# Ending and beginning each stage of a diffusion transformer in two token halves

## The chip, the cores and the metric

The kernel runs on one core of one Trainium2 chip. The metric is the device time of one execution in microseconds (us). The core's engines work side by side from queues of their own, each in order: TensorE (PE in the profile, its weight loads PEld), VectorE (DVE), ScalarE (ACT), GpSimd (POOL), and SyncE (SP), which issues the DMAs. They meet at semaphores.

## The reference

Two layers over 512 latent tokens `h` and 256 context tokens `hc`, 1024 features each. Every layer has three residual stages, and each begins with an RMS norm over the features, scaled and shifted by vectors that a product with `w_ada` gives:

```python
h  = h + 0.5 * g1 * swiglu(modulate(rms_norm(h, p['g_ffn1']), s1, sc1), w1_gate, w1_up, w1_down)
qa, ka, va, qb, kb, vb, uf = split_mixer_inputs(modulate(rms_norm(h, p['g_mix']), s2, sc2) @ p['w_in'])
o  = concatenate([window_attention(...), global_attention(...), fourier_mix(uf, w_four)]) @ p['w_out']
h  = h + g2 * o
h  = h + 0.5 * g3 * swiglu(modulate(rms_norm(h, p['g_ffn2']), s3, sc3), w2_gate, w2_up, w2_down)
# the same for hc, except that after the last layer's mixer only h goes on; the result is rms_norm(h, g_final)
```

## The kernel before

Activations lie with features on the partitions and tokens in the columns: `h`, `xh` and `xl` are 128 partitions x 8 feature blocks (KD) x 768 tokens (TOK: 512 latent, SEQ, then 256 context). For accuracy every product is made of three in a rounded format: a value is its rounded part (`xh`, `whi`, `ah`) plus the rest (`xl`, `wlo`, `al`), and hi x hi, lo x hi and hi x lo are added up in PSUM (`product`, L1234). For one feature block and 768 tokens that is six matmuls: 512 and 256 columns, three times. Each has its own weight load.

There are six stages n = 0 to 5: ffn1, mix, ffn2 in each layer. An ffn stage has two groups g. A group makes 11 pairs of gate and up tiles (8 feature blocks each) and then 8 down tiles d (11 blocks each). A mixer makes 12 tiles of `w_in`, the Fourier part and attention, and 8 tiles of `w_out`. The last stage, and `w_out` of the second layer, work on 512 tokens only. PSUM has two accumulators `ring[0]` and `ring[1]` for these tiles in turn, `side` for small things and two banks. `slot_free` makes TensorE wait until the tile two before has been read.

Weights come through two slots. SP loads `raw` (`load_w`, L319), ACT rounds it to `whi` (`split_hi`, L585) once the product that used the slot has ended (`mm_done`), VectorE makes `wlo` (`split_lo`, L886). After each down or `w_out` tile VectorE adds it to `h` (`residual`, L979), ACT squares the new block (`square`, L604) and GpSimd adds squares up in `acc` (`sum_squares`, L447; the last block is left to TensorE).

A stage's norm stands between the last tile and the next stage's first pair: TensorE sums acc and the last square over the partitions with one-column fp32 matmuls (`sum_chunks`, L1253), ACT takes the root, VectorE the inverse and lays it on diagonals (`norm`, L934; ACT's part is L610), TensorE spreads them to all partitions by a product with ones (`spread_rstd`, L1262), and for each of 8 blocks VectorE makes `t1` (L967), ACT adds the shift and rounds to `xh` (L632), VectorE makes `xl` (L975). `product_pair` (L1238) takes the first two tiles together, block by block as `x_ready` allows, and both end with the last block. In an ffn stage the third tile's split waits for that end. In a mixer the small `wf` products (L1129) and head squares (L1062) follow the pair; `wf` is zeroed by GpSimd and loaded by SP once the whole of x is made (L343 to L348), for it lies where `t1` was.

The `ada` work (L592, L892, L1270) makes the modulation vectors of later stages in 84 halves of units. Plan puts them in slots of ffn stages 0, 2 and 3: a slot is one pair or one down tile (L99 to L108). `gates` (L923) turns a part of them into the factors that `residual` uses.

## Time and profile before

| | us |
|---|---|
| median of 3 runs (2939.7 to 2941.72) | 2941.56 |
| the profiled execution | 2938.7 |
| its span, first to last instruction | 2936.9 |
| TensorE busy | 2764.7 (94%) |
| VectorE, ScalarE, GpSimd busy | 1506.7, 1005.9, 669.7 |

The mean granted clock of TensorE is 0.976 of its full rate. A matmul's duration in the trace holds the time to pass through the array, so matmuls overlap, and the distance of two starts is what one costs in a row.

### The profile page before, as it was taken

What the parts mean: (1) busy time and instruction counts of PE and PEld (TensorE: products, weight loads), DVE (VectorE), ACT (ScalarE), POOL (GpSimd) and SP (SyncE); (2) the same over time, 40 slices, a digit from 0 to 9 for tenths busy, and PEclk for the clock granted to TensorE, in tenths of its full rate; (3) what the DMA queues carried; (4) which work ended last, traced back from release to release, by engine and by line L of the source; (5) the groups of instructions that cost most, each with busy time, mean ns of one, the idle gap of its engine ahead of it and who ended that gap; (6) DMA issues with size and microseconds to landing.
All of it is one profiled execution on the core that took longest, in us unless ns stands there. A gap on an engine that the chain in (4) does not pass through costs nothing.

```text
span 2936.9 us, 36842 instructions
## 1 busy us (share of the span) xinstructions
PE 2764.7 (94%) x14988; PEld 2333.2 (79%) x14988; DVE 1506.7 (51%) x2075; ACT 1005.9 (34%) x1569; POOL 669.7 (23%) x563
## 2 busy tenths in 40 slices
PE   6999999999877889999999899999998987899998
PEld 2888888878656778888888788888887766788886
DVE  1556655664387455565557555422224577433333
ACT  2333333333376333332334333111213366322231
POOL 1233323433033212343325132100011223100001
PEclk8999999989999989999999999999998999999999
DMA  5333333414320123333333233212212520233232
GB/s 214 101 107 132 110 111 108 133 50 157 99 48 15 37 69 115 113 127 109 101 122 115 75 104 111 78 51 65 66 64 78 160 51 1 65 100 108 84 104 78
DMA packets 69432, 274.34 MB, mean 93 GB/s; under 512 B 8592, under 2 KB 9872, under 8 KB 68240
## 3 DMA queue, kind: packets, MB, share of 16 engines
q1 hardware_dynamic: 69264, 271.99, 29.2%
q8 instruction: 119, 1.95, 0.3%
q14 instruction: 49, 0.40, 0.0%
HBM read 258.85 MB, written 13.11 MB: 93 GB/s over the span
## 4 chain that ended last, share of the span: by engine, by line
PE 88%; DVE 6%; ACT 3%; issue 2%; DMA 1%; SPq 0%; POOL 0%; DVEq 0%; ACTq 0%; POOLq 0%
PE ring L1234 74%; PE ring L1248 3%; PE bank L1196 2%; PE side L1177 2%; PE side L1109 1%; PE bank L1301 1%; ACT pth L672 1%; PE bank L1192 1%; PE bank L1280 1%; DVE rstd L882 1%; DVE rstd L880 1%; DVE wlo L889 1%; PE ring L1158 1%; DVE ptl L869 1%; PE ring L1163 1%
## 5 line engine op out<-in xcount | busy, mean ns | idle before, releaser
L1234 PE MATMUL ring<-xh,whi 128*128 128x512 f32 x2808 | 788.4, 349 | 19.5 <-DVE wlo L889 15.9
L1234 PE MATMUL ring<-xh,wlo 128*128 128x512 f32 x2808 | 785.1, 348 | 0.0
L1234 PE MATMUL ring<-xl,whi 128*128 128x512 f32 x2808 | 783.0, 347 | 0.0
L889 DVE TENSOR_TENSOR wlo<-raw,whi 128x1024 fp32r<-128x1024 f32 (+1 forms) x280 | 390.7, 1395 | 551.7 <-ACT whi L590 551.6
L1234 PEld LDWEIGHTS ring<-xh,whi 128*128 128x128 f32 x2808 | 447.0, 189 | 92.9 <-issue 19.1
L1234 PEld LDWEIGHTS ring<-xl,whi 128*128 128x128 f32 x2808 | 446.1, 189 | 70.6
L1234 PEld LDWEIGHTS ring<-xh,wlo 128*128 128x128 f32 x2808 | 446.1, 189 | 70.2
L445 POOL TENSOR_TENSOR ada_acc<-ada_acc,ada_tmp 128x384 f32<-128x384 f32 x252 | 336.1, 1334 | 529.2 <-ACT ada_tmp L602 508.7
L590 ACT ACTIVATE whi<-raw 128x1024 fp32r<-128x1024 f32 (+1 forms) x280 | 314.4, 1123 | 208.1 <-PE ring L1234 208.1
L906 DVE SCALAR_TENSOR_TENSOR ada_acc<-ada_buf,scond,ada_acc 128x384 f32<-128x384 f32 x294 | 353.5, 1203 | 7.1
L1234 PE MATMUL ring<-ah,whi 128*128 128x512 f32 x1232 | 340.8, 346 | 0.0
L1234 PE MATMUL ring<-ah,wlo 128*128 128x512 f32 x1232 | 339.3, 345 | 0.0
L1234 PE MATMUL ring<-al,whi 128*128 128x512 f32 x1232 | 339.1, 345 | 0.0
L728 ACT ACTIVATE ah<-atmp 128x768 fp32r<-128x768 f32 (+1 forms) x88 | 69.8, 793 | 536.6 <-DVE atmp L1021 536.6
L983 DVE SCALAR_TENSOR_TENSOR h<-ring,vec_gate,h 128x512 f32<-128x512 f32 (+1 forms) x136 | 82.0, 637 | 297.1 <-PE ring L1234 297.0
L1234 PEld LDWEIGHTS ring<-ah,wlo 128*128 128x128 f32 x1232 | 195.3, 188 | 28.9
L1234 PEld LDWEIGHTS ring<-al,whi 128*128 128x128 f32 x1232 | 195.2, 188 | 28.9
L1234 PEld LDWEIGHTS ring<-ah,whi 128*128 128x128 f32 x1232 | 195.4, 188 | 28.0
L602 ACT ACTIVATE ada_tmp<-ada_buf,scond 128x384 f32<-128x384 f32 x336 | 188.6, 605 | 73.2 <-POOL ada_acc L445 40.1
L1021 DVE TENSOR_TENSOR atmp<-sil,ring 128x768 f32<-128x768 f32 (+1 forms) x88 | 78.1, 887 | 260.1 <-PE ring L1234 260.1
L724 ACT ACTIVATE sil<-ring 128x768 f32<-128x768 f32 (+1 forms) x88 | 66.7, 758 | 406.3 <-PE ring L1234 391.5
L442 POOL TENSOR_TENSOR ada_acc<-ada_tmp 128x384 f32<-128x384 f32 x42 | 82.7, 1970 | 370.4 <-ACT ada_tmp L602 277.2
(133 smaller groups left out, 2514.4 us busy)
## 6 DMA issues: line engine op xcount, KB each, us to landing
raw<-w_gu SPq DMA_DIRECT2D x176, 512.0 KB, 3.5
ada_buf<-w_ada SPq DMA_DIRECT2D x84, 768.0 KB, 4.2
raw<-w_down SPq DMA_DIRECT2D x64, 704.0 KB, 4.0
...
```

What stands on the lines that cost most here:

```text
L442: pool.tensor_tensor(ada_acc[:, 1], ada_tmp[:, 0], ada_tmp[:, 1], ALU.add).then_inc(ada_ctx_done, 2)
L445: pool.tensor_tensor(ada_acc[:, 1], ada_acc[:, 1], ada_tmp[:, k % 2], ALU.add).then_inc(ada_ctx_done, 1)
L590: act.activation(whi[:, slot, 0:nk * P], raw[:, slot, 0:nk * P], ACT.Copy).then_inc(whi_ready, 1)
L602: act.activation(ada_tmp[:, k % 2], ada_buf[:, k], ACT.Copy, scale=scond[:, 1, k:k + 1]).then_inc(ada_prod_done, 1)
L724: act.activation(sil[:, 0:width], ring[0][:, 0:width], ACT.Silu).then_inc(silu_done, 1)
L728: act.activation(ah[:, f, 0:width], atmp[:, 0:width], ACT.Copy).then_inc(ahi_done, 1)
L889: dve.tensor_tensor(wlo[:, slot, 0:nk * P], raw[:, slot, 0:nk * P], whi[:, slot, 0:nk * P].bitcast(F32), ALU.subtract).then_inc(wlo_ready, 1)
L906: dve.scalar_tensor_tensor(out=ada_acc[:, 0], in0=ada_buf[:, k], scalar=scond[:, 0, k:k + 1], in1=ada_acc[:, 0], op0=ALU.mult, op1=ALU.add ...
L983: last = dve.scalar_tensor_tensor(out=h[:, d, a:b], in0=ring[slot][:, a:b], scalar=vec_gate[:, c, d:d + 1], in1=h[:, d, a:b], op0=ALU.mult ...
L1021: dve.tensor_tensor(atmp[:, 0:width], sil[:, 0:width], ring[1][:, 0:width], ALU.mult).then_inc(prod_done, 1)
L1234: last = pe.matmul(out[:, a:b], w, x[:, k, a:b], start=(i == 0 and m == 0), stop=(i == nk - 1 and m == 2))
L1248: last = pe.matmul(ring[u][:, a:b], w, x[:, k, a:b], start=(k == 0 and m == 0), stop=(k == KD - 1 and m == 2))
```

## The change

`halves(width)` divides the tokens into two parts, each with its columns in `side` and `ring` and its modulation: 512 and 256 of 768, or 256 and 256 of 512.

The last two down or `w_out` tiles (d = 6, 7) are made by `last_products`: first halves of both, then second halves of both. The first half's residual, squares and sum run on their own. TensorE's sum of the first half is placed inside the second half of d = 6 (at block 5, or 4 for `w_out`) and the spread inside that of d = 7 (at block 0, or 2). The second halves are added to `h` by `late_residual`, their squares made by `late_square`, inside the next norm.

The norm takes the halves one after the other. `rstd` is now the inverse along rows of ones, turned by `pe.transpose` instead of spread by a product. The next stage's first weights are split inside the norm: tile t ahead of `t1`, tile t+1 ahead of `t1` of block 4. ACT's table load for Silu comes between the halves. `product_pair` makes the first halves of its two tiles with blocks in turn (tile 0 blocks 0 to 3, then tile 1 and tile 0 alternately), with the second half's sum and spread between them; then the second half of tile 0, then that of tile 1. In the first pair of an ffn stage the third tile's `split_hi` stands ahead of Silu. `gates` is moved to the middle of the stage that uses it, and 11 of the ada halves leave the last down tiles of stages 0 and 2 for stage 3. The final norm and its output are made in two halves as well, with 16 output DMAs in place of 8. SP's and GpSimd's waits for x count 16 steps a stage (X_STEPS) in place of 8.

The core of the diff; the removed lines are those of the functions printed above, and are left out here except for the plan's:

```diff
+def halves(width):
+    return [(0, SEQ, 0, 0), (SEQ, TOK, SEQ, 1)] if width == TOK else [(0, SEQ // 2, 0, 0), (SEQ // 2, SEQ, SEQ, 0)]
+WHOLE = KD - 2
+SQ_STEPS, ACC_STEPS, X_STEPS = WHOLE + 4, WHOLE + 2, 2 * KD
...
-                    edge = (g, slot) in ((0, 0), (GROUPS - 1, GF + KD - 1))
-                    if not edge and len(self.ada_slots) < halves:
+                    edge = (g, slot) == (0, 0) or g == GROUPS - 1 and slot >= GF + (3 if n == 0 else 0)
+                    if not edge and len(self.ada_slots) < parts:
...
             def sum_squares(n, width, ds=range(KD - 1)):
                 for d in ds:
...
+                    for p, (a, b) in enumerate([(0, width)] if d < WHOLE else [(a, b) for a, b, _, _ in halves(width)]):
+                        pool.wait_ge(sq_done, SQ_STEPS * n + d + 1 + 2 * p)
+                        if d == 0:
+                            if n > 0:
+                                pool.wait_ge(ssq_ready, 2 * n)
+                            pool.tensor_copy(acc[:, a:b], sq[:, 0, a:b]).then_inc(acc_done, 1)
+                        else:
+                            pool.wait_ge(acc_done, ACC_STEPS * n + d)
+                            pool.tensor_tensor(acc[:, a:b], acc[:, a:b], sq[:, d % 2, a:b], ALU.add).then_inc(acc_done, 1)
...
+            def std(n, width, p):
+                a, b, o, _ = halves(width)[p]
+                act.wait_ge(ssq_ready, 2 * n + p + 1)
+                act.activation(rms[:, a // P:b // P], side[:, o:o + (b - a) // P], ACT.Sqrt, bias=eps[:],
+                               scale=1.0 / D_MODEL).then_inc(std_done, 1)
+            def widen(n, width):
+                a, b, _, _ = halves(width)[1]
+                act.wait_ge(inv_done, 2 * n + 2)
+                for m in range(a // P, b // P):
+                    last = act.activation(rstd[:, m * P:(m + 1) * P], ones[:], ACT.Copy, scale=rms_inv[:, m:m + 1])
+                last.then_inc(rwide[1], 1)
+            def norm(n, width, layer, stage, resid=None):
+                def late_square(d):
+                    if resid is not None:
+                        act.wait_ge(resid_done, resid + d + 1)
+                        square(n, d, *halves(width)[1][:2])
+                std(n, width, 0)
                 if layer is None:
+                    late_square(KD - 2)
+                    late_square(KD - 1)
+                    std(n, width, 1)
+                    widen(n, width)
                     return
...
+                if n > 0:
+                    split_hi(stages[n]["t"], 0, KD)
+                late_square(KD - 2)
                 act.wait_ge(vec_ready, 2 * (n + 1))
...
+                for p, (a, b, _, c) in enumerate(halves(width)):
+                    for d in range(KD):
+                        if p == 0 and d == 3:
+                            late_square(KD - 1)
+                            split_hi(stages[n]["t"] + 1, 1, KD)
+                        if p == 0 and d == 6:
+                            std(n, width, 1)
+                            widen(n, width)
+                        act.wait_ge(t1_ready, X_STEPS * n + KD * p + d + 1)
                         col = MODC * layer + 3 * KD * stage + d
...
+                        act.activation(xh[:, d, a:b], t1[:, d % 4, a:b], ACT.Identity, bias=modv[:, c, col:col + 1]).then_inc(mod_done, 1)
+                    if p == 0 and stage != 1:
+                        act.preload_act_table(ACT.Silu)
...
+            def square_after(s, before, n, d, ow):
+                if d < WHOLE:
+                    act.wait_ge(resid_done, s["resid"] + before + d + 1)
+                    square(n + 1, d, 0, ow)
+                else:
+                    act.wait_ge(part_resid, 2 * n + d - WHOLE + 1)
+                    square(n + 1, d, 0, halves(ow)[0][1])
...
                             split_hi(tt + 1, 1, KD)
+                        else:
+                            split_hi(tt + 2, 0, nk_next)
...
+            def invert(n, width, p):
+                a, b, _, _ = halves(width)[p]
+                dve.wait_ge(std_done, 2 * n + p + 1)
+                dve.reciprocal(rms_inv[:, a // P:b // P], rms[:, a // P:b // P]).then_inc(inv_done, 1)
+            def norm(n, width, layer, stage, before=None):
                 if layer is not None:
...
                     col = MODC * layer + 3 * KD * stage
+                    units = -(-(col + 2 * KD) * P // ADA_COLS)
+                    dve.wait_ge(ada_red_done, 2 + 4 * (units - FIRST_UNITS))
                     for c in range(2):
                         dve.scalar_tensor_tensor(out=vec_scale[:, c], in0=modv[:, c, col + KD:col + 2 * KD], scalar=1.0,
                                                  in1=gain[:, 3 * layer + stage], op0=ALU.add, op1=ALU.mult).then_inc(vec_ready, 1)
...
                     dve.wait_ge(vec_ready, 2 * (n + 1))
...
+                invert(n, width, 0)
+                dve.wait_ge(inv_done, 2 * n + 1)
+                for m in range(halves(width)[0][1] // P):
+                    last = dve.tensor_scalar(rstd[:, m * P:(m + 1) * P], ones[:], rms_inv[:, m:m + 1], None, ALU.mult)
+                last.then_inc(rwide[0], 1)
+                if before is not None:
+                    late_residual(before, KD - 2)
                 if layer is None:
...
+                    late_residual(before, KD - 1)
+                    invert(n, width, 1)
+                    for p, (a, b, o, _) in enumerate(halves(width)):
+                        dve.wait_ge(rstd_spread[p], n + 1)
+                        for d in range(KD):
+                            dve.scalar_tensor_tensor(out=h[:, d, a:b], in0=h[:, d, a:b], scalar=gain_final[:, d:d + 1],
+                                                     in1=side[:, o:o + b - a], op0=ALU.mult, op1=ALU.mult).then_inc(out_ready, 1)
                     return
...
+                if n > 0:
+                    split_lo(stages[n]["t"], 0, KD)
+                for p, (a, b, o, c) in enumerate(halves(width)):
+                    base = X_STEPS * n + KD * p
+                    dve.wait_ge(rstd_spread[p], n + 1)
+                    for d in range(KD + 1):
+                        if p == 0 and d == 3 and before is not None:
+                            late_residual(before, KD - 1)
+                        if p == 0 and d == 4:
+                            split_lo(stages[n]["t"] + 1, 1, KD)
+                        if p == 0 and d == 6:
+                            invert(n, width, 1)
+                        if d < KD:
+                            if d >= 4:
+                                dve.wait_ge(x_ready, base + d - 3)
+                            dve.scalar_tensor_tensor(out=t1[:, d % 4, a:b], in0=h[:, d, a:b], scalar=vec_scale[:, c, d:d + 1],
+                                                     in1=side[:, o:o + b - a], op0=ALU.mult, op1=ALU.mult).then_inc(t1_ready, 1)
+                        if d >= 1:
+                            e = d - 1
+                            dve.wait_ge(mod_done, base + d)
                             shift = MODC * layer + 3 * KD * stage + e
...
+                            dve.scalar_tensor_tensor(out=xl[:, e, a:b], in0=t1[:, e % 4, a:b], scalar=modv[:, c, shift:shift + 1],
+                                                     in1=xh[:, e, a:b].bitcast(F32), op0=ALU.add, op1=ALU.subtract).then_inc(x_ready, 1)
...
+            def early_residual(n, d, slot, width):
+                a, b, o, c = halves(width)[0]
+                dve.wait_ge(part_done, 2 * n + d - WHOLE + 1)
+                dve.scalar_tensor_tensor(out=h[:, d, a:b], in0=ring[slot][:, o:o + b - a], scalar=vec_gate[:, c, d:d + 1],
+                                         in1=h[:, d, a:b], op0=ALU.mult, op1=ALU.add).then_inc(part_resid, 1)
+            def late_residual(before, d):
+                t0, r0, width = before
+                a, b, o, c = halves(width)[1]
+                dve.wait_ge(mm_done, t0 + d + 1)
+                dve.scalar_tensor_tensor(out=h[:, d, a:b], in0=ring[(r0 + d) % 2][:, o:o + b - a], scalar=vec_gate[:, c, d:d + 1],
+                                         in1=h[:, d, a:b], op0=ALU.mult, op1=ALU.add).then_inc(resid_done, 1)
...
+            def part_product(k, out, slot, nk, xs_hi, xs_lo, part):
+                a, b, o, _ = part
+                w_h, w_l = whi[:, slot, k * P:(k + 1) * P], wlo[:, slot, k * P:(k + 1) * P]
+                for m, (w, x) in enumerate(((w_h, xs_hi), (w_h, xs_lo), (w_l, xs_hi))):
+                    last = pe.matmul(out[:, o:o + b - a], w, x[:, k, a:b], start=(k == 0 and m == 0), stop=(k == nk - 1 and m == 2))
+                return last
+            def last_products(n, tt, r, nk, xs_hi, xs_lo, width, at):
+                first, second = halves(width)
+                for d in (KD - 2, KD - 1):
+                    slot_free(pe, r + d)
+                    pe.wait_ge(wlo_ready, tt + d + 1)
+                    for k in range(nk):
+                        last = part_product(k, ring[(r + d) % 2], (tt + d) % 2, nk, xs_hi, xs_lo, first)
+                    last.then_inc(part_done, 1)
+                for d in (KD - 2, KD - 1):
+                    for k in range(nk):
+                        if d == KD - 2 and k == at[0]:
+                            sum_chunks(n + 1, width, 0)
+                        if d == KD - 1 and k == at[1]:
+                            spread_rstd(n + 1, width, 0)
+                        last = part_product(k, ring[(r + d) % 2], (tt + d) % 2, nk, xs_hi, xs_lo, second)
+                    last.then_inc(mm_done, 1)
+            def product_pair(n, tt, r, width):
+                first, second = halves(width)
+                second_in_row = (second[0], second[1], second[0], second[3])
+                order = [(0, 0), (0, 1), (0, 2), (0, 3)]
+                for k in range(KD):
+                    order.append((1, k))
+                    if k + 4 < KD:
+                        order.append((0, k + 4))
+                for i, (u, k) in enumerate(order):
+                    if n > 0 and i == 3:
+                        sum_chunks(n, width, 1)
+                    if i == 8:
+                        spread_rstd(n, width, 1)
+                    if k == 0:
+                        slot_free(pe, r + u)
+                        pe.wait_ge(wlo_ready, tt + u + 1)
+                    if u == 0:
+                        pe.wait_ge(x_ready, X_STEPS * n + k + 1)
+                    part_product(k, ring[u], u, KD, xh, xl, first)
                 for u in range(2):
...
+                    for k in range(KD):
+                        if u == 0:
+                            pe.wait_ge(x_ready, X_STEPS * n + KD + k + 1)
+                        last = part_product(k, ring[u], u, KD, xh, xl, second_in_row)
+                    last.then_inc(mm_done, 1)
+            def sum_chunks(n, width, p):
+                a, b, o, _ = halves(width)[p]
+                pe.wait_ge(acc_done, ACC_STEPS * n + WHOLE + 1 + p)
+                pe.wait_ge(sq_done, SQ_STEPS * n + WHOLE + 2 + 2 * p)
+                for i, m in enumerate(range(a // P, b // P)):
+                    pe.matmul(side[:, o + i:o + i + 1], acc[:, m * P:(m + 1) * P], ones[:, 0:1], start=True, stop=False)
+                    last = pe.matmul(side[:, o + i:o + i + 1], sq[:, (KD - 1) % 2, m * P:(m + 1) * P], ones[:, 0:1], start=False, stop=True)
                 last.then_inc(ssq_ready, 1)
...
+            def spread_rstd(n, width, p):
+                a, b, o, _ = halves(width)[p]
+                pe.wait_ge(rwide[p], n + 1)
+                for i, m in enumerate(range(a // P, b // P)):
+                    last = pe.transpose(side[:, o + i * P:o + (i + 1) * P], rstd[:, m * P:(m + 1) * P], ident[:])
+                last.then_inc(rstd_spread[p], 1)
...
+                    for d in range(KD if g < GROUPS - 1 else WHOLE):
                         slot_free(pe, r + d)
                         down(t + d, d % 2)
                         ada_turn(plan.ada.get((n, g, GF + d)))
+                    if g == GROUPS - 1:
+                        last_products(n, t, r, GF, ah, al, ow, (5, 0))
                     t += KD
                     r += KD
...
+                if n + 1 == len(stages):
+                    sum_chunks(n + 1, ow, 1)
+                    spread_rstd(n + 1, ow, 1)
```

## Rows read from the trace of the kernel before

**Rows 1.** Part 1 of the page: engine, busy time, share, instructions.
```profile
PE 2764.7 (94%) x14988; PEld 2333.2 (79%) x14988; DVE 1506.7 (51%) x2075; ACT 1005.9 (34%) x1569; POOL 669.7 (23%) x563
```

**Rows 2.** Chain of waits in order of time: start, duration (us), engine, tile, line.
```profile
86.75 34.15 PE ring L1234 x192
...
633.19 1.15 DVE h L983 x2
...
669.83 5.97 PE ring L1234 x24
...
1051.34 1.15 DVE h L983 x2
...
1085.67 35.67 PE ring L1234 x192
...
1121.99 33.28 PE ring L1234 x192
...
1669.45 35.09 PE ring L1234 x192
...
2542.01 0.76 DVE h L983
...
2568.57 170.67 PE ring L1234 x744
```

**Rows 3.** The same chain, window from 630 to 670: the norm's steps.
```profile
635.70 0.22 PE side L1259 x2
...
640.12 0.27 ACT rms L616
...
640.72 0.89 DVE rstd L952 x4
...
641.64 2.08 PE side L1265 x2
```

**Rows 4.** Timeline: start, duration, engine, line; norm on 512 tokens, six transposes.
```profile
2543.56 0.35 PE L1258 MATMUL side<-ones,acc 128*128 128x1 f32 x2 [1.60 <-ACT sq L608]
...
2550.39 1.41 DVE L967 SCALAR_TENSOR_TENSOR t<-h,vec_scale,side 128x512 f32<-128x512 f32 x2 [2.17 <-PE side L1265]
...
2552.89 0.77 PE L1248 MATMUL ring<-xh,whi 128*128 128x512 f32 x1 [2.53 <-DVE xl L975]
...
2254.69 0.82 PE L1070 MATMUL side<-ident,rstd 128*128 128x128 f32 x6
```

**Rows 5.** Windows: length, busy of each engine (instructions), PEclk, DMA share, GB/s.
```profile
636.00:637.00 1.00, 1.00 (x7) 1.00 (x6) 0.75 (x1) 0.15 (x1) 0.00 (x0) 0.50 0.00 0
...
653.00:654.00 1.00, 1.00 (x8) 0.87 (x8) 1.00 (x3) 0.91 (x2) 0.00 (x0) 1.00 0.00 0
...
867.00:870.00 3.00, 1.08 (x5) 0.69 (x5) 2.52 (x7) 1.97 (x7) 0.51 (x1) 1.00 0.00 0
```

**Rows 6.** Chain of waits between the pair and the third tile.
```profile
1083.21 1.06 ACT whi L590
...
1084.29 1.24 DVE wlo L889
```

**Rows 7.** Timeline of VectorE and GpSimd during w_out.
```profile
1020.43 2.02 DVE L889 TENSOR_TENSOR wlo<-raw,whi 128x1024 fp32r<-128x1024 f32 x1 [1.86 <-ACT whi L590]
...
1019.53 1.85 POOL L457 TENSOR_TENSOR acc<-acc,sq 128x768 f32<-128x768 f32 x1 [6.63 <-ACT sq L608]
```

**Rows 8.** Groups by line: busy us, mean ns of one, idle before.
```profile
L626 ACT ACT_TABLE_LOAD x4 | 5.1, 1283 | 0.1
```

**Rows 9.** SP's timeline, and DMA issues with KB and us to landing.
```profile
661.82 2.44 SPq L348 DMA_DIRECT2D wf<-w_four  x4
...
wf<-w_four SPq DMA_DIRECT2D x4, 16.0 KB, 2.7
```

**Rows 10.** Groups by line: VectorE's ada accumulations.
```profile
L906 DVE SCALAR_TENSOR_TENSOR ada_acc<-ada_buf,scond,ada_acc 128x384 f32<-128x384 f32 x294 | 353.5, 1203 | 7.1
```

**Rows 11.** Chain of waits at the end of the last product.
```profile
2921.72 0.76 DVE h L983
```

207 lines of the change are left out of this document (68 added, 139 removed).

## The prediction

> **What bounds the kernel now.** TensorE is busy for 94% of the span [rows 1], so I read first where it is not. The chain of waits, in order of time, is, outside attention (which the change leaves alone), one string of product stretches, broken for long at one kind of place: where a stage ends, the next one's norm must be made, and the pair of first tiles can't start before it. [rows 2] hold those places. I take an interval "gap plus pair" from the last product's end (the residual L983 starts 0.03 us later) to the first matmul of the stage's third tile (L1234): 36.7 us into the first mixer (633.16 to 669.83), 34.4 after it (1051.31 to 1085.67), and likewise 34.0 between the layers (to 1669.45) and 36.2 into the second mixer, whose beginnings repeat the pattern and are not shown; 26.6 into the last stage (2541.98 to 2568.57). Five in all. The pair itself is 96 matmuls. 192 matmuls take 33.28 us [rows 2], so 96 cost 16.6; at 512 columns each one costs 170.67/744 = 0.229, hence 0.117 for one of 256. Some 17 us of each interval are therefore not products.
>
> What fills them: residual and square to the first norm sum, 1.6 us (2541.98 to 2543.56); 24 one-column matmuls; root, inverse and diagonal, 1.5 us from 640.12 to 641.61; two fp32 broadcasts, the first 2.08; then t1, xh and xl before the pair [rows 2 to 4]. All of it is serial. The clock adds to it: it is at 0.50 of 2.4 GHz (the 1.2 GHz level) from 636, 2.8 us after the products' end, until 653, well into the pair [rows 5]. After the pair the third tile waits for its own weights, 1.06 of ACT and 1.24 of VectorE [rows 6], because both slots come free together; and the 192 matmuls behind that wait take 35.67 and 35.09 us instead of 33.28 [rows 2]: 2.4 and 1.8 more at the lower level, 0.9 at the start.
>
> **The change, part by part.** T is the start of product d=6 of the last group, M the end of its second half, s the start of t1(0).
>
> *Last products.* The same columns in another order: 33 x 0.229 = 7.6 us for each first half, then 33 x 0.117 = 3.9 for each second (24: 5.5 and 2.8 for w_out). That the 256-column matmuls, which now follow one another with a fresh weight load each, keep 0.117 is an inference from the alternating pattern; between its nearest rows, the 0.117 and the 0.137 of a transpose with 128 columns (0.82/6 [rows 4]), I take 0.117, since in the pattern one load always lies under such a matmul. At 0.137 the five boundaries lose 5 x 100 x 0.02 = 10 us; that end stays in the range.
>
> *Norm of the first half.* It is ready to be summed 1.6 + 0.16 (drain) us after T+15.1, at T+16.9; the sum stands at k=5, T+16.87, so no stall (with w_out at k=4: 0.35 us). It is 16 instructions at 0.11 (0.22 for two [rows 3]) = 1.8 us; new on TensorE's path. M = T+15.1+1.8+3.9 = T+20.8. Root to widened rstd is the 1.5 us of [rows 3], under the remaining 18 matmuls (2.1 us). The broadcast becomes 4 transposes, 0.45 us at 0.11, where 2.08 stood. So d=7 ends at T+25.1 against T+22.9 before.
>
> *What is late next.* After M, in each queue's order: ACT rounds the next tile's weights (1.06), VectorE takes late_residual(6) beside it, then split_lo (1.24), then t1. GpSimd's half add falls on that split_lo. With such an add (1.85) beside it the same line took 2.02 us instead of 1.24 [rows 7]; an add of 256 columns is a third, 0.62, so 0 to 0.6 more; I take 0.6. So s = M + 0.2 + 1.06 + 1.24 + 0.6 = M+3.0, T+23.8. From t1(0) to the first pair matmul is 2.50 us at 512 columns [rows 4], that is T+26.3: a stall of 1.2 us behind d=7 (2.7 for w_out, whose second half is shorter). VectorE then needs 0.66 (two in 1.41, one in 0.76 [rows 2, 4]) twice per k, 1.32, plus late_residual(7) 0.39 (1.15 less 0.76 [rows 2]) and behind it ACT's square and split, on which VectorE's split_lo waits (1.2 with the wait), and the inverse 0.2. x of k=0 to 7 is ready at s + 2.5, 3.8, 5.5, 8.2, 9.5, 11.0, 12.35, 13.25.
>
> *Pair.* TensorE's units (tile, k) of first halves cost 0.69. (0,0), (0,1), (0,2) follow x, the second sum (0.9) lies behind (0,2), (0,3) starts at s+8.2; the remaining 12 units and two transposes run without a wait to s+17.4. Second halves: ACT's table load of 1.28 [rows 8] now stands between the halves (not for a mixer), x is then made each 0.79 us and its last comes at s+21.2 (mixer s+19.9), so tile 0 ends s+21.6 and tile 1 at s+24.4 (mixer 23.05). The third tile's weights are split from s+21.9 to 24.2, under tile 1: the wait that was there goes, and with it the slow 192 matmuls.
>
> *Mixer.* The zeroed wf is loaded only when all x are made: its issues take 2.44 us from 0.4 after the last x, and the last lands 2.7 later [rows 9]. So wf is there about s+25.1 and L1129 waits 2.1 us where today the pair hides it. The chan products and head squares (2.3) follow as before.
>
> *Moved with it.* Eleven ada halves leave the last products of stages 0 and 2 for stage 3: the same 6 transposes per unit on TensorE, VectorE's 4 accumulations of 1.2 us [rows 10] under pairs of 16.6; cost 0, and 4.8 us per half where VectorE were late. gates now sits ahead of the down products: 0.24 us under them. SP queues the loads of the third and fourth tile behind the later split_lo of the pair's, but they are needed at s+21.9 and later, so 15 us stand over: 0.
>
> **The sum.** Intervals after, less the old product time: between layers 48.2-22.9 = 25.3 (before 34.0, and 1.8 of slow matmuls): 10.5 saved. From the first mixer M = T+16.0, s = T+19.0, end T+43.4, less 16.6: 26.8, before 34.4+2.4: 10.0. Into the mixers 23.8+25.1+2.3-22.9 = 28.3: 8.4 and 7.9. Into the last stage, all 256 wide: the weights of d=7 are ready 1 us late (T+3.8 against 2.8), the second x are paced by ACT and VectorE, interval 22.4: 4.2. At the start one split fewer ahead of the norm and the cheaper broadcast put t1(0) at 60.3 instead of 62.5; the third tile at 83.9 instead of 86.75, and 0.9: 3.8. At the end 15.2 us from 2921.70 to 2936.9 [rows 11] become 1.9 within the products and 11.7 behind: 1.6. Total 46.4.
>
> Against it, the clock. Between T+25.1 and s+8.9 TensorE has about 4 us of waits in five pieces, and a sum of one-column matmuls. A stretch of attention with 1.08 us busy of 3 kept 1.00 [rows 5]; a single wait of 2.3 us ahead of 1085.67 was followed by 0.50. Both can happen. One fall costs 0 where x is late anyway and 1.5 us where it lasts to s+12, since tile 1 then runs behind; over five boundaries 0 to 7.5, and I take 4.4. Saving 42.0. The profiled execution, 2938.7, becomes 2896.7; it lay 2.9 under the median of the runs, so for that median 2941.56 - 42.0 = 2899.6.
>
> The Trainium skill speaks against this design here: TensorE: Matmul & The Clock Gate, "A second HAM failure mode: psum-queue depth-cycling", says that frequent short idles between groups of matmuls make the clock swing and cost throughput even if no idle is long. By it every pair would pay, which is the first rival; the row of attention does not agree, the row of 1085.67 does.
>
> **Rivals.** (1) *The clock falls at each pair's start and stays down while the two tiles take turns.* For: the slow matmuls behind a 2.3 us wait. Against: the steady 1.00 in attention. Price: 8.5 us of first halves at half rate from s+5.5 to s+14, 4.2 us more per pair, 21 in all in place of the 4.4: 2916. (2) *All of the norm is covered.* Floor of an interval: 16.6 + 2.7 of sums + 0.65 of transposes (+2.3). For: the sums are that. Against: VectorE's 2.5 us to the first x has no product left to lie under. Saves about 80: 2862. (3) *Slower: the 1.8 us of one-column sums inside product d=6 drop the clock there, and it doesn't come back before the third tile.* The second halves left then take 51 x 0.096 = 4.9 more, the pair 14 to 16 more, and slower sums: 17.5 a boundary, 88 in all, 2983. It decides from 9.3 us lost a boundary. For: the fall at 636 comes during such sums. Against: they stood behind a wait of 2.2 us there, and continuous products brought the clock back by 653. (4) *It doesn't do what it says*: an order of waits in which VectorE's in-order queue (split_lo of the second tile waits on ACT's late square, and t1(4) behind it) keeps the pair until the old time. Price: 8 us a boundary given back: about no change, 2938.
>
> **Chances.** Forecast 0.74, own range 2890 to 2909; rival 1 0.15; rival 2 0.03; rival 3 0.04; rival 4 0.04. A measurement of this kernel tells 0.2% (5.9 us) from no change. Faster 0.92 (first three), same 0.04, slower 0.04. The range takes in the load at 0.137, rival 1 and the case without clock loss: 2887 to 2920.
>
> **What would show it.** In the profile after: matmuls of 256 columns at starts 0.117 apart in the last products; a wait of 1 to 3 us, not 14, between them and the pair; no L889 wait ahead of the third tile, and 192 matmuls behind it in 33.3; a wait of some 2 us ahead of the wf products; granted clock of the last products 1.00. It is wrong if pair starts lie more than 5 us behind the last product, if the clock stays at 0.50 through the pairs, or if the third tile still waits for its weights.

## The result, and the profile after

The changed kernel takes 2893.51 us (median of 4 runs, 2892.9 to 2899.59), the kernel before 2940.63 beside it (2935.83 to 2941.72): a ratio of 0.985, 95% interval 0.983 to 0.9865. The forecast was 2899.6, range 2887 to 2920: a saving of 42.0 us; 47.1 came by these medians, 44.8 by the two profiled spans (2936.9 and 2892.1).

TensorE does 176 matmuls more than in [rows 1] and is busy 15 us less. I put that down to the two broadcasts a stage (2.08 and 0.87 us) that went and to less time at the lower clock: the mean granted clock of the profiled execution is 0.984, before 0.976. The changed kernel, part 1 of the page:

```profile
PE 2749.7 (95%) x15164; PEld 2333.0 (81%) x15164; DVE 1503.0 (52%) x2106; ACT 1015.9 (35%) x1602; POOL 676.7 (23%) x570
```

The chain of waits of the changed kernel, in order of time (start, duration, engine, tile, line; L1328 is the half product, L1319 the whole one, L1044 the residual that starts 0.03 us after the product before d = 6 ends). It answers [rows 2]: at each boundary the first line is the start T of product d = 6, and the L1319 line behind it the first matmul of the next stage's third tile.

```profile
83.83 33.92 PE ring L1319 x192
...
607.69 17.14 PE ring L1328 x81
...
658.41 5.66 PE ring L1319 x24
...
1020.84 10.94 PE ring L1328 x48
...
1063.82 33.92 PE ring L1319 x192
...
1098.40 33.28 PE ring L1319 x192
...
1586.06 17.14 PE ring L1328 x81
...
1635.59 16.96 PE ring L1319 x96
...
2155.91 17.14 PE ring L1328 x81
...
2201.94 3.39 DMA wf<-w_four
...
2207.97 4.25 PE ring L1319 x12
...
2490.51 0.76 DVE h L1044
...
2524.52 170.44 PE ring L1319 x744
...
2862.04 0.76 DVE h L1044
```

Less the old product time, as in the forecast's sum (the first and last rows are whole), the intervals in us are (with what the matmuls behind the third tile's start gave back, now 33.92 us for 192, or 16.96 for 96, where [rows 2] have 34.15, 35.67 and 35.09):

| place | before | forecast | measured | saved: forecast | saved: measured |
|---|---|---|---|---|---|
| start (third tile) | 86.75 | 83.9 | 83.8 | 3.8 | 2.9 + 0.2 |
| into mixer 1 | 36.7 | 28.3 | 27.8 | 8.4 | 8.9 |
| after mixer 1 | 34.4 + 2.4 | 26.8 | 26.3 | 10.0 | 8.1 + 1.8 |
| between the layers | 34.0 + 1.8 | 25.3 | 26.6 | 10.5 | 7.4 + 1.2 |
| into mixer 2 | 36.2 | 28.3 | 29.2 | 7.9 | 7.0 |
| into the last stage | 26.6 | 22.4 | 23.2 | 4.2 | 3.4 |
| from T to the end | 30.6 | 29.0 | 30.1 | 1.6 | 0.5 |
| the clock | | | in the rows above | -4.4 | |
| sum | | | | 42.0 | 41.4 |

The other 3.4 us of the 44.8 lie between these places, in the mixers and the long product stretches, which vary from run to run by about as much (last section).

Where an interval's time went, between the layers, the changed kernel's timeline (in brackets the idle time before and what ended it); it answers [rows 3, 4, 7]:

```profile
1607.03 0.60 PE L1391 MATMUL side<-ident,rstd 128*128 128x128 f32 x4
1607.23 0.48 DVE L1060 SCALAR_TENSOR_TENSOR h<-ring,vec_gate,h 128x256 f32<-128x256 f32 x1 [0.77 <-PE ring L1328]
1607.29 1.06 ACT L602 ACTIVATE whi<-raw 128x1024 fp32r<-128x1024 f32 x1 [2.02 <-PE ring L1328]
...
1608.39 1.23 DVE L938 TENSOR_TENSOR wlo<-raw,whi 128x1024 fp32r<-128x1024 f32 x1 [0.67 <-ACT whi L602]
...
1608.74 1.47 POOL L469 TENSOR_TENSOR acc<-acc,sq 128x256 f32<-128x256 f32 x1 [12.15 <-ACT sq L620]
...
1609.53 1.40 DVE L1031 SCALAR_TENSOR_TENSOR t<-h,vec_scale,side 128x512 f32<-128x512 f32 x2
...
1612.02 0.47 PE L1328 MATMUL ring<-xh,whi 128*128 128x512 f32 x1 [0.53 <-DVE xl L1037]
...
1622.07 1.28 ACT L667 ACT_TABLE_LOAD   x1
1623.98 0.38 PE L1391 MATMUL side<-ident,rstd 128*128 128x128 f32 x2
1624.40 0.87 DVE L1031 SCALAR_TENSOR_TENSOR t<-h,vec_scale,side 128x256 f32<-128x256 f32 x2 [1.56 <-PE side L1391]
```

The first half's norm is done (spread at 1607.03) by the time d = 6 ends (1607.2, T+21.1). s, the start of t1(0), is 1609.53, T+23.5; the first pair matmul waits 0.53 us at s+2.5. The second half's t1 waits 1.56 us for a spread that comes at s+14.5.

The granted clock in windows of the changed kernel (length, busy time of PE, PEld, DVE, ACT, POOL with instructions, PEclk, DMA share, GB/s), which answers [rows 5]. The last products run at 1.00; the pair between the layers and those at 2187 and 2508 fall to 0.50; after mixer 1 the clock falls while d = 7 runs, 1.4 us behind the one-column sums of 1033.4 to 1035.2, and once more in the pair:

```profile
1586.00:1616.00 30.00, 28.42 (x165) 24.12 (x164) 13.76 (x23) 9.05 (x13) 4.62 (x3) 1.00 0.18 62
1617.00:1623.00 6.00, 5.38 (x13) 4.27 (x14) 5.44 (x9) 4.55 (x8) 0.00 (x0) 0.50 0.27 87
...
1036.80:1040.00 3.20, 3.20 (x17) 3.20 (x16) 2.43 (x4) 1.36 (x2) 1.47 (x1) 0.50 0.01 3
...
2187.00:2190.00 3.00, 2.52 (x6) 2.03 (x7) 2.73 (x6) 2.17 (x6) 0.00 (x0) 0.50 0.57 175
2508.00:2514.00 6.00, 5.51 (x27) 5.42 (x26) 5.03 (x11) 4.11 (x9) 0.00 (x0) 0.50 0.24 87
```

The end, where [rows 11] had one line and the final scaling behind it, on the changed kernel's timeline:

```profile
2880.56 0.35 PE L1382 MATMUL side<-ones,acc 128*128 128x1 f32 x2 [1.12 <-ACT sq L620]
...
2881.99 6.34 DVE L1013 SCALAR_TENSOR_TENSOR h<-h,gain_final,side 128x256 f32<-128x256 f32 x16
2882.54 7.72 SPq L417 DMA_DIRECT2D out<-h  x16
```

### The profile page after: what moved, and what is told of

The parts are those of the page before. It is cut to its first block, busy times and chain, and to the rows that moved or that the text cites. A ratio compares the mean times of both kernels' runs of the same rounds, so it can differ in the third digit from the quotient of the medians.

```text
span 2892.1 us, 37299 instructions
## 1 busy us (share of the span) xinstructions
PE 2749.7 (95%) x15164; PEld 2333.0 (81%) x15164; DVE 1503.0 (52%) x2106; ACT 1015.9 (35%) x1602; POOL 676.7 (23%) x570
## 3 DMA queue, kind: packets, MB, share of 16 engines
q1 hardware_dynamic: 70416, 271.99, 30.1%
## 4 chain that ended last, share of the span: by engine, by line
PE 87%; DVE 7%; ACT 3%; issue 2%; DMA 1%; SPq 1%; POOL 0%; DVEq 0%; ACTq 0%; POOLq 0%
PE ring L1319 72%; PE ring L1328 5%; PE bank L1280 2%; PE side L1261 2%; PE side L1193 1%; PE bank L1426 1%; ACT pth L719 1%; PE bank L1404 1%; DVE wlo L938 1%; PE bank L1276 1%; DVE xl L1037 1%; DVE t L1031 1%; DVE rstd L931 1%; DVE rstd L929 1%; PE ring L1242 1%
## 5 line engine op out<-in xcount | busy, mean ns | idle before, releaser
L1319 PE MATMUL ring<-xh,whi 128*128 128x512 f32 x2760 | 772.7, 348 | 8.6 <-DVE wlo L938 5.0
L1319 PE MATMUL ring<-xh,wlo 128*128 128x512 f32 x2760 | 767.1, 346 | 0.0
L1319 PE MATMUL ring<-xl,whi 128*128 128x512 f32 x2760 | 766.9, 346 | 0.0
L1319 PEld LDWEIGHTS ring<-xh,whi 128*128 128x128 f32 x2760 | 438.4, 189 | 77.4 <-issue 6.3
L1319 PEld LDWEIGHTS ring<-xl,whi 128*128 128x128 f32 x2760 | 438.4, 189 | 68.4
L1319 PEld LDWEIGHTS ring<-xh,wlo 128*128 128x128 f32 x2760 | 437.4, 188 | 68.6
L1319 PE MATMUL ring<-ah,whi 128*128 128x512 f32 (+1 forms) x1078 | 297.9, 346 | 0.0
L1319 PE MATMUL ring<-al,whi 128*128 128x512 f32 (+1 forms) x1078 | 296.6, 344 | 0.0
L1319 PE MATMUL ring<-ah,wlo 128*128 128x512 f32 (+1 forms) x1078 | 296.5, 344 | 0.0
L1044 DVE SCALAR_TENSOR_TENSOR h<-ring,vec_gate,h 128x512 f32<-128x512 f32 x116 | 69.9, 637 | 258.3 <-PE ring L1319 258.2
L1319 PEld LDWEIGHTS ring<-ah,wlo 128*128 128x128 f32 x1078 | 170.9, 188 | 25.3
L1319 PEld LDWEIGHTS ring<-al,whi 128*128 128x128 f32 x1078 | 170.8, 188 | 25.3
L1319 PEld LDWEIGHTS ring<-ah,whi 128*128 128x128 f32 x1078 | 170.7, 188 | 24.8
```

The source lines that it names most:

```text
L1044: last = dve.scalar_tensor_tensor(out=h[:, d, a:b], in0=ring[slot][:, a:b], scalar=vec_gate[:, c, d:d + 1], in1=h[:, d, a:b], op0=ALU.mult ...
L1319: last = pe.matmul(out[:, a:b], w, x[:, k, a:b], start=(i == 0 and m == 0), stop=(i == nk - 1 and m == 2))
```

## The experiments

Kernels of a few us' difference can't be ranked by medians here: one kernel's runs lie up to 16 us apart. So each is also read by its *places*: the third tile's start in the first stage, plus T to the third tile at the five boundaries, plus T to the end, from its profiled execution. The changed kernel: 83.7 + 50.7 + 43.0 + 49.5 + 52.1 + 34.0 + 30.2 = 343.3 (the first by its matmul's own start, 83.7; the chain counts it from 83.83). The sums scatter too. Between the layers e3 and e6 leave everything as it is, and their profiles show 47.3 there where the changed kernel's shows 49.5. So a difference in the sum of places of less than about 3 us tells nothing by itself, and has to be found at the place that the edit touches.

| kernel | median | ratio to before (95%) | places | against the changed kernel |
|---|---|---|---|---|
| changed kernel | 2893.5 | 0.9848 (0.983 to 0.9865) | 343.3 | |
| e1_norm_after | 2912.7 | 0.9923 (0.9898 to 0.9948) | 368.9 | +25.6 |
| e2_pairs | 2927.7 | 0.9968 (0.9956 to 0.998) | 369.9 | +26.6 |
| e3_wf_early | 2888.9 | 0.984 (0.9814 to 0.9865) | 341.3 | -2.0 |
| e4_fill | 2893.1 | 0.9851 (0.9829 to 0.9873) | 349.0 | +5.7 |
| e5_spread_early | 2898.5 | 0.9859 (0.9838 to 0.988) | 344.9 | +1.6 |
| e6_two_queues | 2895.3 | 0.9848 (0.9827 to 0.9868) | 341.4 | -1.8 |
| e8_sum_on_pe | 2895.2 | 0.9854 (0.9829 to 0.9879) | 345.4 | +2.1 |
| e9_t1_before | 2895.1 | 0.9848 (0.9828 to 0.9869) | 343.7 | +0.4 |
| e10_light_fill | 2889.9 | 0.9828 (0.9804 to 0.9851) | 339.1 | -4.2 |
| e11_all | 2880.2 | 0.98 (0.978 to 0.982) | 332.1 | -11.2 |
| e12_silu_first | 2897.7 | 0.986 (0.9837 to 0.9883) | 346.5 | +3.2 |
| e13_sums_twice | 2906.9 | 0.9896 (0.988 to 0.9913) | 358.6 | +15.3 |

**What the overlap is worth: e1_norm_after.** In `last_products`:

```diff
-                        if d == KD - 2 and k == at[0]:
-                            sum_chunks(n + 1, width, 0)
-                        if d == KD - 1 and k == at[1]:
-                            spread_rstd(n + 1, width, 0)
...
                     last.then_inc(mm_done, 1)
+                sum_chunks(n + 1, width, 0)
+                spread_rstd(n + 1, width, 0)
```

> One part undone: the first half's sum of squares and its spreading come after the second halves of both last products, not between them; all else stays as in the changed kernel. Theory (the norm under the products is what pays): in the changed kernel t1(0) starts 23.46 us after T (T is the start of product d=6 of the last group) into the mixers and between the layers, 18.4 after the mixer, 13.2 in the last stage. Undone, T to the last matmul of the products is 22.9, then 1.8 of sums, 2.9 of root, inverse, widening and spreading, so t1(0) at about T+28.1, T+22.0 and T+20: later by 4.6 three times, 3.6 and 6.5, with 0.5 at the end: about +24 us, 2917 to 2919. Rival (the first pair is bound by VectorE's own work from t1(0) on, and the late residual, split and second sum that now lie behind t1(0) go in front of it instead): VectorE has about 2 us of that work, so +2 to +3 a place, about +12, 2905.

T to s grew by 4.2 at three places (theory 4.6) and by 2.9 and 3.0 after the mixers (theory 3.6 and 6.5; the last was worked out with 11 blocks a tile where w_out has 8), and the end by 2.2. The medians say +19, the places +25.6, the theory +24, the rival +12. The chain between the layers, all in line behind the products:

```profile
1592.12 23.09 PE ring L1328 x132
...
1617.51 0.88 DVE rstd L1003 x4
1618.38 0.39 DVE h L1060
1618.77 1.13 DVE wlo L938
1619.90 0.67 DVE t L1031
```

The mechanism is the theory's at 4.2 of its 4.6 us in three places; the 2.9 and 3.0 after the mixers are also what the rival gives a place. So some 20 of the change's 45 us are the first half's norm under the second halves.

**The turns: e2_pairs.** In `product_pair`, with the second sum at i = 6 and its spread at 12, and the second halves likewise in pairs:

```diff
-                order = [(0, 0), (0, 1), (0, 2), (0, 3)]
-                for k in range(KD):
-                    order.append((1, k))
-                    if k + 4 < KD:
-                        order.append((0, k + 4))
+                order = [(u, k) for k in range(KD) for u in range(2)]
```

> The turns undone: the first pair's products are taken as (tile 0, k), (tile 1, k) in both halves, with the second sum and the spread put where as many blocks of x are needed as now; the halves of the norm stay. Theory (the last block of x, 21.2 us after t1(0), sets the end, and the third tile's split of 1.06 and 1.23 us lies either under tile 1 or behind both): both tiles end at s+21.9, the third tile starts at s+24.3 where it now starts at s+24.4 to s+26: 0 us, within 2 either way, in the ffn stages; the mixers, which wait for w_four, gain up to 1 each. Rival (the turns keep TensorE fed, and without them it falls behind the blocks of x): +1 to +2 at each of 6 places, about +8, 2901.

My theory was wrong and the rival too small: +26.6 by the places, +34 by the medians. The edit undoes two things, the head start in the first halves and the order tile by tile in the second, and both cost. The timeline of e2_pairs between the layers:

```profile
1632.44 1.23 DVE L938 TENSOR_TENSOR wlo<-raw,whi 128x1024 fp32r<-128x1024 f32 x1
...
1633.82 0.77 PE L1328 MATMUL ring<-xh,whi 128*128 128x512 f32 x1 [3.44 <-DVE wlo L938]
...
1656.12 0.59 PE L1319 MATMUL ring<-xh,whi 128*128 128x512 f32 x2 [2.20 <-DVE wlo L938]
```

Tile 1's weights are split only ahead of t1(4), and unit (1, 0) now stands second in TensorE's queue: it waits 3.4 us, the following units pile up, the second sum moves from s+6.2 to s+12 and its spread from s+12 to s+17. The pairs' last matmuls start at s+25.3 to s+26.7 (s+22.6 in the last stage), where the theory had the pair's end at s+21.9. Up to there the places take 10.0 us more than in the changed kernel, 1.1 of them ahead of the first pair, which the edit leaves alone.

The other 16.6 us lie behind the pair's last matmul. With both tiles ending together nothing covers the third tile's weights: at the four places that lead into an ffn stage TensorE waits 2.2 us for them, and the third tile comes 2.4 us later behind the pair than it did. In the mixers it comes 2.2 and 5.0 us later; in mixer 2 TensorE waits 4.5 us for w_four with nothing over it. The theory had counted the wait for the weights and missed the pair's beginning. So the head start of four units and the second halves one tile after the other are the change's second main part, and of the two the order of the second halves is worth more by these numbers.

**The clock: e4_fill and e10_light_fill.** Idle matmuls in TensorE's waits; e10 leaves out those of the second half:

```diff
                     if u == 0:
+                        fill({1: 4, 2: 4, 3: 8}.get(k, 0))
                         pe.wait_ge(x_ready, X_STEPS * n + k + 1)
...
+            def fill(count):
+                for _ in range(count):
+                    pe.matmul(bank[0][:, 0:2 * P], whi[:, 0, 0:P], whi[:, 0, 0:2 * P], start=True, stop=True)
```

> Matmuls that compute nothing used (256 columns, from the weights in place to a bank that is free) are put into TensorE's waits in the first pair: 4, 4 and 8 ahead of blocks 1, 2 and 3 of x in the first half and 3 ahead of each block in the second. They take 0.12 us each at full clock, 16 x 0.12 = 1.9 us of waits of 0.5 to 1.9 each that are there anyway. Theory (the clock's falls during the pair cost what stands in the rows: second spread late by 1.56 us between the layers and 0.58 us in the last stage, slow matmuls behind): the granted clock stays at 1.00 in 1616 to 1624, 1046 to 1050, 2187 to 2190 and 2508 to 2514, and the kernel gains 1.5+0.6+1+1 = about 4 us, 2889.5. Rival a (the blocks of x set the time and TensorE at half speed keeps up): clock up but 0 us. Rival b (the fill delays the pair): +0.3 to +0.5 at each place, +2 to +3.

> As in e4_fill, but the idle matmuls stand in the first half of the pair only (4, 4 and 8 ahead of blocks 1, 2 and 3 of x); the second half has none. Theory (in e4_fill the clock stayed up and the second half's 21 fills, 21 x 0.117 = 2.5 us, put the pair's end from s+23.7 to s+26.1, where TensorE and no longer the blocks of x is the bound; s is the start of t1(0)): here the clock stays up through 8 blocks and the pair ends at s+23.7 everywhere, which the changed kernel reached at 1 place of 5: -0.9 at three places and -2.3 between the layers, about -4 us against 2893.5. Rival (the fills in the second half were what kept the clock up, or those in the first half cost as much as they bring): falls of 3.4 us and more remain in the pairs, 0.

In e4 the clock stayed up in all five pairs behind the first stage's and the wait for the second spread went (between the layers the last t1 ends at s+19.2, not s+20.8). But the 21 fills of the second half put the end of four pairs at s+26.1: rival b, at 2.4 us a place for the 0.3 to 0.5 expected. The last stage's pair, at s+20.6, lost nothing. In e10 it stayed up as well (after mixer 1 it still fell ahead of s, behind the sums), and the pairs end at s+23.7, 23.8, 23.8, 23.7 and 20.5, against 23.7, 24.6, 26.1, 24.6 and 20.8. Windows over those pairs in e10 (columns as above); the changed kernel's mean clock over its own two pairs is 0.87 and 0.91:

```profile
1613.00:1637.00 24.00, 23.14 (x142) 20.06 (x141) 20.37 (x38) 16.03 (x25) 0.73 (x1) 1.00 0.24 77
1044.80:1069.00 24.20, 22.87 (x138) 19.74 (x137) 20.59 (x38) 16.02 (x25) 0.66 (x1) 1.00 0.24 77
```

The theory held, at its size: against e10 the changed kernel's pairs end 0 + 0.8 + 2.3 + 0.9 + 0.3 us later, and the first one 0.4: 4.7. That is one profile. In e3, e6, e8, e12 and e13, whose pairs are made in the same way, the same sum is 2.7 to 4.2, as the falls come in other pairs and last 3.4 or 6.8 us: between the layers there is none in e3, e6 and e12. What held in every profile is that no pair behind the first stage's had a fall with the fill (15 pairs, in e4, e10 and e11), while 29 of 40 had one in the eight kernels that keep the turns and have no fill.

**Do one-column sums bring the clock down? e13_sums_twice.**

```diff
-                for i, m in enumerate(range(a // P, b // P)):
+                for i, m in list(enumerate(range(a // P, b // P))) * (2 if p == 0 and n > 0 else 1):
```

> The first half's one-column sums are made twice over in the last products of every stage (16 matmuls more, 8 in the last two places; the second go gives the same values). Theory (they stand on the path to t1(0) through M, the end of d=6's second half, and cost their own time and no more, as the clock did not fall in or after them into the mixers and between the layers): T to t1(0) grows by 1.8 us at four places and 0.9 at one, 0.9 at the end: +9, 2902.5. Rival (the recorded rival 3, in which one-column matmuls within the products bring the clock down until the third tile): the clock reads 0.50 from d=7 to the third tile where it now read 1.00 at T+15 to T+24, and a place costs 10 us or more: +40 and over, 2935.

T to s grew by 2.9, 3.6, 4.8, 4.7 and 0.9: more than the 1.8 and 0.9 of the matmuls themselves. Windows and chain of e13 between the layers:

```profile
1605.00:1607.00 2.00, 2.00 (x20) 1.97 (x18) 0.00 (x0) 0.02 (x1) 0.00 (x0) 1.00 0.00 0
1607.50:1614.00 6.50, 6.50 (x32) 6.50 (x32) 1.05 (x5) 0.26 (x1) 0.00 (x0) 0.50 0.00 0
1615.00:1617.00 2.00, 2.00 (x20) 2.00 (x19) 1.74 (x2) 0.54 (x2) 1.39 (x1) 1.00 0.00 0
```

With 32 one-column matmuls (1605.2 to 1610.0) the clock fell at three boundaries where with 16 it had not, though TensorE was busy throughout. It fell while they ran, so the last of them were slow too, and the 18 half matmuls behind them took 4.06 us for 2.23. It was back by 1615. So both expectations failed in part: the mechanism of rival 3 exists, but it lasts 3 to 7 us and costs 1 to 3, not 17.5.

**The port: e8_sum_on_pe.** GpSimd's last add goes, TensorE sums that block too:

```diff
+                    if p == 1:
+                        pe.matmul(side[:, o + i:o + i + 1], sq[:, 0, m * P:(m + 1) * P], ones[:, 0:1], start=False, stop=False)
```

> GpSimd's last addition of each norm (second half, block 6) is left out and TensorE sums that block itself, with 2 one-column matmuls more (4 at the end of the last stage's kind, as the second half has 2 chunks everywhere: 2 each). So nothing of GpSimd lies beside VectorE's split of the first weights. The prediction's term (the addition holds the split up by 0.6 us at 5 places, so t1(0) at T+24.2): the kernel gains 5 x 0.6 = 3.0 us. Rival, from the trace of the changed kernel (the split of 1.23 us starts first and is not held up, it is the addition that takes 1.47 us for 0.74): t1(0) stays at T+23.63, T+18.5 and T+13.4, and the time within 0.5 us of the changed kernel's, 2893.5.

s stayed at T+23.6 three times, and at T+18.9 and 13.4; with no add beside it the split takes the 1.23 us that it took with it:

```profile
1605.59 1.23 DVE L938 TENSOR_TENSOR wlo<-raw,whi 128x1024 fp32r<-128x1024 f32 x1 [0.67 <-ACT whi L602]
1606.73 1.40 DVE L1031 SCALAR_TENSOR_TENSOR t<-h,vec_scale,side 128x512 f32<-128x512 f32 x2
```

The rival holds: the term of 0.6 us was nothing. (T+18.9 for 18.5 is no loss by the edit: after mixer 1, s lies between T+18.5 and T+19.7 in the profiles that leave that place alone.)

**w_four: e3_wf_early.** The zeroing and the four loads come before the waits for x; the rope table stays behind:

```diff
-                    sp.wait_ge(x_ready, X_STEPS * (n + 1))
-                    sp.dma_start(rope_tab[:], rope).then_inc(tab_loaded, 16)
                     sp.wait_ge(wf_zeroed, layer + 1)
...
+                    sp.wait_ge(x_ready, X_STEPS * (n + 1))
+                    sp.dma_start(rope_tab[:], rope).then_inc(tab_loaded, 16)
...
-                    pool.wait_ge(x_ready, X_STEPS * (n + 1))
```

> One wait moved: w_four's tile is zeroed by GpSimd before the norm's blocks of x are ready and its 4 loads are issued ahead of SyncE's wait for the last block of x; the rope table's load stays behind that wait. Theory (in the mixers the wait for w_four ends last): TensorE waited 0.85 us for it in mixer 1 and up to 3.4 us in mixer 2, so -4 us, 2889.5, with the third tile at T+26.9 and T+25.9 in place of 27.8 and 29.2. Rival (another wait, for the copy out of tile 0 or for the third tile's split, ends at almost the same time): -1 us or nothing.

From the pair's end to the third tile it is 2.0 us at both mixers, where it was 3.4 and 3.9: 1.4 and 1.9 us of waits went, less than the 4 expected, as more than half of mixer 2's 3.39 in the chain lay under the pair (to 2203.97). The medians are 4.6 us apart, and the four runs of e3 (2887.5 to 2892.0) lie clear of the changed kernel's. The chain of e3 in mixer 2 has no wait between the pair and the third tile:

```profile
2189.95 10.54 PE ring L1327 x69
2200.49 0.89 PE bank L1212 x8
2201.39 1.24 PE side L1145 x12
2202.62 2.87 PE ring L1318 x12
```

**VectorE's order: e9_t1_before.** t1(0) is moved ahead of `late_residual(before, KD - 2)` and `split_lo(stages[n]["t"], 0, KD)`.

> VectorE's order changed at the start of each norm but the first: t1(0), which needs only the first spread, comes ahead of block 6's late residual and of the split of the first weights, not behind them. Theory (VectorE is the bound from t1(0) to the last block of x, and waits idle for the end of d=6 just before): t1(0) moves from T+23.63 to T+21.6, and the rest of the norm and the third tile by the 0.75 us that t1(0) takes, to 1.2 where the first product was waiting for it: -0.75 to -1.2 at 5 places, about -4.5 us, 2889. Rival (TensorE's own work, 24 us of matmuls in the pair at s+2.5 to s+24, is the bound, or the clock takes it back): 0 to -1.

s came to T+21.8 at three places as expected, and x of block 1 at T+26.7 instead of T+27.7. But the second spread still came behind the eighth unit, at s+13.2 to s+14.5, and the pairs ended at T+47.9 with a fall of the clock (48.5 in e3, mixer 2) and at T+46.7 without (47.4 in e10): 0.6 us where 0.75 was expected, and after the mixers nothing, since there the weights' split was late, not t1. Sum of places +0.4: not told from nothing.

**The spread's place: e5_spread_early.**

```diff
-                    if i == 8:
+                    if i == 6:
                         spread_rstd(n, width, 1)
...
-                        if p == 0 and d == 6:
+                        if p == 0 and d == 5:
                             std(n, width, 1)
```

> One thing moved: the second half's root, inverse and widening stand one block of x earlier (ahead of block 5, not 6), and TensorE spreads it after 6 blocks of products, not 8. Theory (a fall of the clock in the pair costs mainly through the second spread, which VectorE waits for: 1.56 us between the layers and 0.58 us in the last stage): those waits go, the second spread comes at s+9 to s+11 instead of s+12 to s+14.5 (s is the start of t1(0)), the last t1 is at s+19.1 everywhere: -1.6, -0.6 and 0.2 at the rest: about -3 us. The table load of 1.28 us between the halves, hidden so far behind the late spread, may then show: up to +0.5 at each of 4 places, so -3 to -1. Rival (the pair's end is set by TensorE at the lower clock, not by the blocks of x): 0.

Between the layers the last t1 ends at s+19.2 (20.8) though the clock fell there as well, and the third tile starts at s+24.5 (25.9); the last stage gains 0.2. That looks like 1.6 us of the 3, but the falls are not alike: it lasted 3.4 us in e5 and 6.8 in the changed kernel. In e8 and e13, with the spread where it was and a fall of 3.4 us at this boundary, the pair ends at s+24.8 and s+24.9; in e5 at s+24.7. Into mixer 1, with such a fall in both, e3 and e5 both end at s+24.8, while the last t1 ends at s+19.5 in e3 and s+19.1 in e5. So with a fall of 3.4 us the earlier spread brings the last block of x forward by 0.3 to 0.4 us and the pair's end by 0.2 at most: that is the rival, the end is set by TensorE at the lower clock. For a fall of 6.8 us only the last stage compares, with 0.2 us of the 0.6. The total is inconclusive.

**The end: e6_two_queues.** ScalarE issues the odd blocks of the second half of the output.

> The 8 stores of the second half of the output are issued in turns by SyncE and ScalarE instead of all 16 by SyncE. Theory (the end is bound by SyncE's issuing, 16 x 0.48 = 7.7 us from 2882.5 to 2890.3, where VectorE makes a block in 0.40 us and is done at 2888.3): the last issue moves to 2888.4, the kernel ends 1.9 us sooner, T to the end 28.3 in place of 30.2. Rival (the last transfers, not their issues, set the end: the 16 engines are shared): 0 to -0.5.

T to the end is 29.4 in place of 30.2: 0.8 of the 1.9. The timeline of e6:

```profile
2884.56 6.33 DVE L1017 SCALAR_TENSOR_TENSOR h<-h,gain_final,side 128x256 f32<-128x256 f32 x16
...
2888.58 2.69 ACTq L653 DMA_DIRECT2D out<-h  x4
```

SyncE was the bound for the last 1.9 us; behind it stood ScalarE, whose issues take 0.67 us each, from block to block of VectorE's.

**The third tile's rounding: e12_silu_first.** In the first pair ScalarE takes Silu first, `split_hi(tt + 2, 0, nk_next)` after it.

> One part undone: in the first pair of every stage but the mixers ScalarE takes tile 0's Silu first and rounds the third tile's weights after it, as before the change; the rest stays. Theory (tile 0 ends about 2.9 us ahead of tile 1, and the rounding of 1.06 and the split of 1.23 us just fit under tile 1): with the Silu of 0.7 to 1.0 us in front, the third tile starts at s+24.9 to s+25.3 in place of s+24.4 in the stages with no late second spread (s is the start of t1(0)): +0.5 to +0.9 at each of 4 places, +2 to +3 in all, 2896. Rival (the pair's end is late for other reasons, the clock among them, and the split has room): 0, with the third tile's start at the pair's end as now.

The third tile starts 0.2 to 0.4 us behind the pair's last matmul where it had started with it (s+24.6, 25.2, 24.2 and 21.0 against 24.2, 24.5, 25.9 and 20.6, the third with the clock up). Counted from the pair's last matmul it is 0.4 to 0.6 us later at each of the four places, 1.9 in all: the theory's mechanism, just under its size of 2 to 3. The medians, 4.2 us apart with runs of e12 that lie 16 us apart, tell nothing.

**All together: e11_all.**

> All that pointed downwards, together: w_four's wait moved (e3), the second spread earlier (e5), t1(0) ahead of the split (e9), the light fill (e10), the second half of the output from two queues (e6), and in the last norm the first half's 8 products made before block 7's late residual, while TensorE still has d=7's second half. Theory (each part takes its own wait away): -3.0 for w_four (1.4 and 1.9 in the traces), -4 for the clock's falls with the second spread, 3 x 0.75 for t1(0), -3.2 for VectorE's 8 x 0.40 at the end and -0.9 for the queue: -13, 2880. Rival (TensorE's own matmuls, some 21 us of them in the pair, become the bound before all of it is had, and the runs differ by 3 us on their own): -6 to -8, 2886.

2880.2 us, 13.3 below the changed kernel and 2% below the kernel before. The pairs run at clock 1.00, T to the third tile is 48.7, 43.5, 46.7, 48.7 and 33.8 (50.7, 43.0, 49.5, 52.1, 34.0), T to the end 26.9. Of the 3.3 us gained there e6 alone gave 0.8; the rest comes from VectorE, which makes the first half's 8 blocks while TensorE is still at d = 7:

```profile
2865.66 3.21 DVE L1016 SCALAR_TENSOR_TENSOR h<-h,gain_final,side 128x256 f32<-128x256 f32 x8
...
2873.18 3.22 DVE L1016 SCALAR_TENSOR_TENSOR h<-h,gain_final,side 128x256 f32<-128x256 f32 x8 [1.26 <-PE side L1401]
```

The pairs now end at s+25.0, 1.2 us longer after s than in e10, so of the 1.9 us by which s is earlier 0.7 reach their end. VectorE accounts for it: block 6's late residual and the split now lie behind t1(0), the last t1 ends at s+20.35 where e10 has s+19.10, and from there to the pair's end it is 4.6 us in both. So with the clock up it is still the blocks of x, and not TensorE's matmuls, that set the pair's end.

## Why the prediction was right, and where its terms were not

**The mechanism** held at every place: the second halves cover the first half's norm, the wait ahead of the pair is 0.53 us where 1.2 was forecast, and with the three behind it (0.3, 0.75 and 0.9) TensorE's waits up to s+8.1 add up to 2.5 us where I had about 4. The third tile waits for nothing in the ffn stages, and the 192 matmuls behind it take 33.92 us. e1, e2 and e12 undo the parts one by one and each gives time back. The saving by places was 41.4 for 42.0 forecast. That it came so close is partly luck: several terms were wrong by 1 to 2 us and cancel.

**Matmuls of 256 columns** cost 0.117 us each, as inferred; the bound of 0.137 (10 us) did not come about.

**s.** Forecast M+3.0, T+23.8; measured T+23.5, made of two errors: M came at T+21.1 instead of T+20.8, and the 0.6 us for GpSimd's add were wrong (e8). The step that failed was reading [rows 7] without its order. There GpSimd had started first and VectorE's line took 2.02 us; here VectorE starts first, takes its 1.23 and the 256-column add takes 1.47 us instead of the 0.74 that it takes alone at 2876.42. So whoever starts second waits, and which one that is changed with the change. The Trainium skill says the same (SBUF — State Buffer, "SBUF: two separate sides"): the shared port pair is held by whichever started first for its whole instruction. The trace agrees with it in both directions.

**The blocks of x** came at s+2.5, 3.7, 5.4 and 8.1 for the forecast's 2.5, 3.8, 5.5 and 8.2. Their last one did not: the table load between the halves was priced at 1.28 us of the pair's path (s+24.4 in an ffn stage against 23.05 in a mixer), yet with the clock up the pairs end at s+23.8 with it and at s+23.7 without. The load at 1622.07 lies under VectorE's wait for the second spread. Pair ends were 0.6 us early in the one kind and late in the other.

**The clock.** 4.4 forecast; 4.7 by e10 against the changed kernel's profile, 2.7 to 4.2 for the same pairs in five other profiles. The size was right, and the account of it partly. The clock fell in four pairs of the five and once ahead of one. What a fall costs is clear for 3.4 us of it: the pair ends 0.8 to 1.1 us later, by TensorE's slow matmuls, since the earlier spread of e5 does not give it back. A fall of 6.8 us costs 0.3 in the last stage and 2.3 between the layers, and there VectorE also waits 1.56 us for the second spread; how the 2.3 divide between the two stays open. The rule of the Trainium skill that the prediction weighed (TensorE: Matmul & The Clock Gate, "A second HAM failure mode: psum-queue depth-cycling"), that frequent short idles make the clock swing, held in part: the falls came, but not in every pair, and e10 removed them with 16 matmuls a pair and gained 4 us, not 21. Rival 1 was right in kind and at least four times too dear; rival 3 occurs in small after mixer 1 and, when doubled, at three places more. Why one pair has a fall and the next has none, with the same waits in both, was not found.

**w_four.** Forecast a wait of 2.1 us at each mixer; e3 shows 1.4 and 1.9.

**After mixer 1 and between the layers** the gain of the matmuls behind the third tile was set too high, at 2.4 and 1.8 for 1.8 and 1.2. The reference of 33.28 us for 192 was wrong for them: the same matmuls run at one of two paces, 33.28 or 33.92 us for 192, at a granted clock of 1.00 (last section). After mixer 1 they have the slower one in both kernels, so 0.6 of the 2.4 us was never the clock's; between the layers they have the faster one before and the slower one after.

**The end.** Forecast 1.6, measured 0.5. Within the products it is 2.0 us for the 1.9 forecast; behind them 12.6 for 11.7. The step that failed is the pricing of those 11.7 us without SyncE's queue: halving the blocks made 16 issues of 0.48 us out of 8 of 0.61, and VectorE's 16 halves at 0.40 stood ready sooner than SyncE took them. e6 frees 0.8 of it; the rest of what the halving could bring was never used, as VectorE began the first half only after the second half's residual (e11: 3.3 us with the second queue).
